# Attention of a hybrid block: one pipeline over pairs of heads, V as the stationary side

## What is computed

```python
scores = einsum('bqhgd,bkhd->bhgqk', qn, keys) - slopes * dist
scores = where(valid, scores, -inf)
m = maximum(max(scores, axis=-1), sink)
p = exp(scores - m)
probs = p / (sum(p, axis=-1) + exp(sink - m))
out = einsum('bhgqk,bkhd->bqhgd', probs, vals)

merged = (sigmoid(gr) * (y_ret @ w_ret_branch) + sigmoid(gs) * (y_swa @ w_swa_branch))
```

## Time and profile before

| | us |
|---|---|
| median of the runs | 1774.69 |
| lowest, highest of 3 | 1774.11, 1777.1 |
| the profiled execution: whole | 1776.14 |
| the profiled execution: first to last instruction (span) | 1774.6 |
| PE busy (share) | 1731.8 (98%) |
| DVE busy | 966.0 (54%) |
| ACT busy | 723.5 (41%) |
| POOL busy | 183.2 (10%) |

### The profile page before, as it was taken

The page is one execution under the profiler, slowest core; times in us unless marked ns, Lnnn a source line. Parts: engine busy times, 40 slices in busy tenths (PEclk is TensorE's granted clock), DMA queues, the critical chain, the costliest instruction groups (busy, mean ns, idle before and its releaser), DMA issues.

```text
span 1774.6 us, 24247 instructions
## 1 busy us (share of the span) xinstructions
PE 1731.8 (98%) x8504; PEld 1434.5 (81%) x8504; DVE 966.0 (54%) x1844; ACT 723.5 (41%) x1519; POOL 183.2 (10%) x329
## 2 busy tenths in 40 slices
PE   7999999999999999999999999879999989999999
PEld 6777888888778888888888788668888878888887
DVE  4311246522366666675556434766666645765776
ACT  5322345423255444444312213555455454444443
POOL 1000010100000000000222100112122122200000
PEclk9999999999999999999999999999999999999999
DMA  5111113211111111111555312244344349843363
GB/s 189 48 48 49 47 57 116 88 63 48 31 53 46 58 43 58 40 63 39 187 176 190 119 60 83 83 135 150 136 171 150 137 156 355 269 158 100 117 193 101
DMA packets 90580, 195.67 MB, mean 110 GB/s; under 512 B 10481, under 2 KB 26929, under 8 KB 90481
## 3 DMA queue, kind: packets, MB, share of 16 engines
q1 hardware_dynamic: 62432, 100.68, 18.0%
q0 software_dynamic: 28048, 93.74, 15.0%
HBM read 139.69 MB, written 54.53 MB: 109 GB/s over the span
## 4 chain that ended last, share of the span: by engine, by line
PE 91%; DVE 4%; DMA 2%; ACT 2%; issue 1%; SPq 0%; ACTq 0%; DVEq 0%
PE bank L585 26%; PE bank L590 26%; PE bank L589 26%; PE bank L848 4%; PE bank L809 2%; PE bank L842 1%; DMA RAW<-in_w_in 1%; DVE WL L1428 1%; PE bank L828 1%; PE bank L830 1%; DVE SOPL L1853 1%; PE bank L765 1%; PE bank L621 0%; PE bank L616 0%; PE bank L713 0%
## 5 line engine op out<-in xcount | busy, mean ns | idle before, releaser
L1428 DVE TENSOR_TENSOR WL<-RAW,WH 128x512 fp32r<-128x512 f32 x152 | 99.5, 688 | 153.3 <-ACT WH L1034 152.5
L585 PE MATMUL bank<-WH,HN 128*128 128x512 f32 x448 | 177.2, 395 | 4.0 <-DVE HN L1453 2.4
L585 PE MATMUL bank<-WH,ADH 128*128 128x512 f32 x448 | 175.4, 392 | 5.6 <-DVE WL L1994 5.6
L590 PE MATMUL bank<-WL,HN 128*128 128x512 f32 x448 | 175.4, 392 | 0.0
L589 PE MATMUL bank<-WH,HN 128*128 128x512 f32 x448 | 175.4, 391 | 0.0
L589 PE MATMUL bank<-WH,ADL 128*128 128x512 f32 x448 | 175.1, 391 | 0.0
L590 PE MATMUL bank<-WL,ADH 128*128 128x512 f32 x448 | 175.0, 391 | 0.0
L585 PE MATMUL bank<-HN,WH 128*128 128x512 f32 x384 | 157.3, 410 | 1.0 <-DVE WL L1428 1.0
L590 PE MATMUL bank<-HN,WH 128*128 128x512 f32 x384 | 150.8, 393 | 0.0
L589 PE MATMUL bank<-HN,WL 128*128 128x512 f32 x384 | 150.3, 391 | 0.0
L1403 ACT CAST ADH<-ARAW 128x512 fp32r<-128x512 f32 x112 | 69.5, 621 | 173.3 <-PE bank L590 171.0
(11 more groups left out here) (281 smaller groups left out, 3744.4 us busy)
## 6 DMA issues: line engine op xcount, KB each, us to landing
ARAW<-uop SPq DMA_DIRECT2D x112, 256.0 KB, 3.4
RAW<-in_w_in SPq DMA_DIRECT2D x104, 256.0 KB, 3.0
WRAW<-in_w_up SPq DMA_DIRECT2D x16, 1024.0 KB, 5.4
uop<-US POOLq DMA_DIRECT2D x64, 256.0 KB, 2.7
gates<-TB POOLq DMA_DIRECT2D x48, 256.0 KB, 2.3
uop<-UA POOLq DMA_DIRECT2D x48, 256.0 KB, 2.3
TH<-gates POOLq DMA_DIRECT2D x32, 256.0 KB, 3.0
RAWD<-in_w_down SPq DMA_DIRECT2D x32, 256.0 KB, 4.2
```

What stands on the lines that cost most here:

```text
L585: mm = pe.matmul(bank, ahi, bhi, start=first, stop=False, skip_group_check=onto)
L590: return pe.matmul(bank, ahi, blo, start=False, stop=last, skip_group_check=onto)
L1428: dve.tensor_tensor(WL[:, k, :], RAW[:, k % 4, :], WH[:, k, :].bitcast(F32), ALU.subtract)\
```

## The change

The attention becomes one pipeline over all 64 pairs of heads (8 blocks of 8), in 67 steps `T`, written out without loops; the 256 dense gate steps are spread evenly, 3 or 4 per step. Pair `T` gets its scores at the end of PE's step `T`, is transposed in step `T+2`, and pairs are multiplied with V in twos (a group of 4 heads) in every even step, two to three steps after.

- Scores and maximum: `tensor_tensor_reduce` (DVE) adds the distance to the scores, scales by the negated slope and takes the minimum with the negated sink in one instruction for each head (and a short one that reads the accumulator). POOL writes the sink beside the scores (`set_sink`), so that ACT's exponential sums it in with the rest. DVE takes the reciprocal, and POOL multiplies the weights by it (`tensor_scalar`, two of 272 columns) before they are transposed.
- Product with V: `KVR` holds V of a head group as 64 high and 64 low channels, 128 stationary columns. The moving side is the transposed weights of 4 heads, 512 columns, as a high part `PTH` (ACT) and a low part `PTL` (DVE), so 2 matmuls for each block of keys, float32r. The meta keys take 2 matmuls of 256 columns, 64 rows.
- y comes with channels on partitions. ACT copies bank 7 to `YA`; SP copies the upper half to its place in `RT`, and an accumulating POOL transfer adds the lower half. The 64 transposes of y are gone.
- Q and K of the next block are transposed group by group (4 and 2 transposes at a time, into bank 5).
- V of all blocks has to be split: a 256-column copy (ACT) and a subtraction (DVE) more in each block.

```diff
+STEPS = NPAIR + 3
+def gate_steps(T):
+    return range(4 * KT * 8 * T // STEPS, 4 * KT * 8 * (T + 1) // STEPS)
...
+            for T in range(STEPS):
+                for slab, k in ((SLAB_D, KT - 1),) if T == 0 else new_slabs(T - 1):
+                    load_block(8 * slab + k + 4)
+                if T >= 4 and T % 2 == 0:
+                    G = (T - 4) // 2
+                    sp.wait_ge(ya_rdy, G + 1)
+                    for par in range(2):
+                        sp.dma_start(y_place(G, par), y_part(G, 0, par)).then_inc(yc_done[G % 2], 16)
+            for slab, k in new_slabs(STEPS - 1):
+                load_block(8 * slab + k + 4)
...
+            def set_sink(T):
+                if T >= 3:
+                    pool.wait_ge(e_rdy, T - 2)
+                p = T % 8
+                pool.tensor_copy(PR[:, T % 3, 0:PRW:PRW - 1], NSK[:, 2 * p:2 * p + 2]).then_inc(sk_set, 1)
...
+            for T in range(STEPS + 2):
+                for i in gate_steps(T - 1) if 1 <= T <= STEPS else ():
...
+                    set_sink(T + 1)
+                if 1 <= T <= NPAIR:
+                    b = (T - 1) % 3
+                    pool.wait_ge(rc_rdy, T)
+                    for hl in range(2):
+                        pr = pool.tensor_scalar(PR[:, b, PR_KEYS[hl]], PR[:, b, PR_KEYS[hl]], RC[:, b, hl:hl + 1], None,
+                                                ALU.mult)
+                    pr.then_inc(pn_rdy, 1)
+                if T >= 6 and T % 2 == 0:
+                    G = (T - 6) // 2
+                    pool.wait_ge(yc_done[G % 2], 32 * (G // 2 + 1))
+                    for par in range(2):
+                        pool.dma_start(y_place(G, par), y_part(G, 1, par), accum_op=ALU.add)\
+                            .then_inc(yf_done[G % 2], 16)
...
+            def transpose_p(pair):
+                n, b = pair // 8, pair % 3
+                pe.wait_ge(pn_rdy, pair + 1)
+                if pair >= 1:
+                    pe.wait_ge(pl_rdy, split_of(pair - 1))
...
+            def values(G):
+                n, g = G // 4, G % 4
+                if G == 0:
+                    pe.wait_ge(mvb_done, 64)
+                pe.wait_ge(ql_rdy, 2 * n + 2)
+                pe.wait_ge(pl_rdy, meta_of(G))
+                if G >= 1:
+                    pe.wait_ge(ya_rdy, G)
+                for par in range(2):
+                    pe.matmul(B[7][:, :].rearrange("p (r a t) -> p r a t", r=2, a=2)[:, :, par, :],
+                              MVB[0:HD, par, g * P:(g + 1) * P],
+                              PTM[0:HD, :].rearrange("p (r t) -> p r t", r=2), start=par == 0, stop=True,
+                              skip_group_check=par == 1)
+                for sl in slots_of(n):
+                    v = KVR[:, n if sl == n % 2 else n - 1, g * P:(g + 1) * P]
+                    for part, tile in enumerate((PTH, PTL)):
+                        mm = pe.matmul(B[7][:, :], v, tile[:, sl, :, :].rearrange("p h t -> p (h t)"), start=False,
+                                       stop=True, skip_group_check=True)
+                mm.then_inc(pv_full, 1)
...
+            for T in range(STEPS):
+                for i in gate_steps(T):
+                    gate_step(i)
+                if T >= 4 and T % 2 == 0:
+                    values((T - 4) // 2)
+                if 2 <= T < NPAIR + 2:
+                    transpose_p(T - 2)
+                if T in NEXT_Q:
+                    transpose_next_q(*NEXT_Q[T])
+                if T in NEXT_K:
+                    transpose_next_k(*NEXT_K[T])
+                if T < NPAIR:
+                    scores(T)
...
+            def take_p(pair):
+                n, G = pair // 8, pair // 2
+                act.wait_ge(pt_full, pair + 1)
+                if pair % 2 == 0 and G >= 1:
+                    act.wait_ge(pv_full, G)
+                act.copy(pair_part(PTH, n, pair), pair_bank(n)).then_inc(ph_rdy, 1)
+                if pair % 2 == 1:
+                    act.copy(PTM[0:2 * META, :], B[6][0:2 * META, 0:2 * P]).then_inc(ph_rdy, 1)
+            def take_y(G):
+                act.wait_ge(pv_full, G + 1)
+                if G >= 2:
+                    act.wait_ge(yf_done[G % 2], 32 * (G // 2))
+                act.copy(YA[G % 2][:, :], B[7][:, :]).then_inc(ya_rdy, 1)
+            def weigh(T):
+                p = T % 8
+                act.wait_ge(sk_set, T + 1)
+                for hl in range(2):
+                    act.wait_ge(nm_rdy, 2 * T + hl + 1)
+                    part = PR[:, T % 3, hl * (NKEY + 1):(hl + 1) * (NKEY + 1)]
+                    e = act.activation(part, part, ACT.Exp, scale=-1.0, bias=NM[:, T % 3, hl:hl + 1],
+                                       accum_out=RS[:, T % 3, hl:hl + 1])
+                e.then_inc(e_rdy, 1)
+            for T in range(STEPS):
+                for i in gate_steps(T):
+                    if i % 8 == 7:
+                        c = i // 8
+                        g = tanh_gate(ACT_D + c, c % 8, 8 + c // 2)
+                        g.then_inc(a_free if c < 16 else th_rdy, 1)
+                if 2 <= T < NPAIR + 2:
+                    take_p(T - 2)
+                if T >= 4 and T % 2 == 0:
+                    take_y((T - 4) // 2)
+                if T % 8 == 2 and T // 8 + 1 < NB:
+                    hi_q(T // 8 + 1)
+                if T % 8 == 3 and T // 8 + 1 < NB:
+                    hi_kn(T // 8 + 1)
+                if T in NEXT_Q:
+                    take_next_q(*NEXT_Q[T])
+                for slab, k in new_slabs(T):
+                    split_hi(slab, k)
+                if T < NPAIR:
+                    weigh(T)
...
+            def top(T):
+                n, p = T // 8, T % 8
+                if p == 0:
+                    dve.wait_ge(dt_full[n % 2], 16 * (n // 2 + 1))
+                if T >= 3:
+                    dve.wait_ge(pt_full, T - 2)
+                for hl in range(2):
+                    hh = 2 * p + hl
+                    dve.wait_ge(sc_full, 2 * T + hl + 1)
+                    dve.tensor_tensor_reduce(PR[:, T % 3, PR_KEYS[hl]], B[2 + hl][:, 0:NKEY], DT[:, n % 2, KEYS_OF[hl]],
+                                             -SLOPES[hh], NSK[:, hh:hh + 1], ALU.add, ALU.min,
+                                             NM[:, T % 3, hl:hl + 1]).then_inc(nm_rdy, 1)
+            def lo_p(pair):
+                n, G = pair // 8, pair // 2
+                dve.wait_ge(ph_rdy, split_of(pair))
+                dve.tensor_tensor(pair_part(PTL, n, pair), pair_bank(n), pair_part(PTH, n, pair).bitcast(F32), ALU.subtract)\
+                   .then_inc(pl_rdy, 1)
+                if pair % 2 == 1:
+                    dve.wait_ge(ph_rdy, meta_of(G))
+                    dve.tensor_tensor(PTM[2 * META:4 * META, :], B[6][0:2 * META, 0:2 * P],
+                                      PTM[0:2 * META, :].bitcast(F32), ALU.subtract).then_inc(pl_rdy, 1)
+            for T in range(STEPS):
+                if T < NPAIR:
+                    top(T)
+                if 2 <= T < NPAIR + 2:
+                    lo_p(T - 2)
+                if T % 8 == 0 and T // 8 + 1 < NB:
+                    normed_qk(T // 8 + 1)
+                if T % 8 == 2 and T // 8 + 1 < NB:
+                    lo_q(T // 8 + 1)
+                if T % 8 == 3 and T // 8 + 1 < NB:
+                    lo_kn(T // 8 + 1)
+                if T in NEXT_K:
+                    take_next_k(*NEXT_K[T])
+                for i in gate_steps(T):
+                    if i % 8 == 7 and i >= 128:
+                        c = i // 8
+                        dve.wait_ge(th_rdy, c - 15)
+                        dve.scalar_tensor_tensor(out=TB[:, c % 2, :], in0=TB[:, c % 2, :], scalar=1.0,
+                                                 in1=B[c % 2][:, :], op0=ALU.add, op1=ALU.mult).then_inc(a_free, 1)
+                for slab, k in new_slabs(T):
+                    split_lo(slab, k)
+                if T < NPAIR:
+                    dve.wait_ge(e_rdy, T + 1)
+                    dve.reciprocal(RC[:, T % 3, :], RS[:, T % 3, :]).then_inc(rc_rdy, 1)
...
-            def transpose_ys(b, u, bank):
-                for k in range(4):
-                    mm = pe.transpose(bank[:, k * P:(k + 1) * P], RT[:, u, b, k * P:(k + 1) * P], IDN[:, :])
-                mm.then_inc(st_full, 1)
...
+            def hi_ys(b, u):
+                for par in range(2):
+                    act.wait_ge(yf_done[par], 32 * (2 * b + u + 1))
                 act.copy(YS[b // 4][:, 0, 4 * u:4 * u + 4, (b % 4) * P:(b % 4 + 1) * P],
-                         bank[:, :].rearrange("p (k t) -> p k t", k=4)).then_inc(sh_rdy, 1)
+                         RT[:, u, b, :].rearrange("p (k t) -> p k t", k=4)).then_inc(sh_rdy, 1)
             for u in range(2):
```

More of the change, by code:

```diff
@@ L47, with new_slabs, split_of, meta_of @@
 START = 1
-KS_D = [[0, 1, 2], [3, 4, 5], [6, 7]]
+NPAIR = 8 * NB
+NG = NPAIR // 2
+STEPS = NPAIR + 3
+NEXT_Q = {8 * (m - 1) + 2 * g + 3: (m, g) for m in range(1, NB) for g in range(4)}
```

(41 more changed lines are left out.)

470 lines of the change are left out of this document (182 added, 288 removed).

## The result

The changed kernel takes 1746.80 us, median of 4 runs (1745.42 to 1747.64), against 1774.54 for the kernel before: ratio 0.984, 95% interval 0.9823 to 0.9857. That is 27.7 us less, where 44.5 were forecast. It lies 0.2 us inside the upper end of the range (1747), and two of the four runs lie beyond it. Its profiled execution has a span of 1744.6 us, 30.0 less.

What follows compares the result with a forecast made beforehand. PE's work was taken to bound the kernel: 1774.7 us, less 58.6 of PE's work, plus 14.1 of waits for other engines, gave 1730.2 us, with a range of 1714 to 1747.

Steps and rivals of the forecast that it cites:

- dearer DVE: Rival, chance 0.20: `tensor_tensor_reduce` takes two cycles a column, 1.6 us a pair, adding 10 us, so 1740.
- Product with V: PE's attention stage: 64 pairs at 1.41 us go, 32 groups at 1.25 come; net -52.0 us.
- Waits: PE waiting for other engines in the attention stage: Q's split, slab changes and small ones, +14.1 us.
- Splitting Q: ACT and DVE finish splitting the next Q after PE wants it, in 7 blocks: 4.5 us of waits.
- Slab changes: Around steps 16, 32 and 48 DVE's extra work makes PE wait: 8.9 us together.
- Scores: A gate matmul now always follows a pair's last score matmul, saving 0.11 us in each of 64: -7.0 us.
- transposes of block 0: Block 0 leaves out two transposes a pair on PE: -1.5 us.
- Q and K pieces: PE's 24 transposes of Q and K a block come in 8 pieces instead of 2: +3.8 us.
- End of the stage: PE idles 6.1 us instead of 4.1 before the branch projection, behind weight tiles and casts of y: +2.0 us.
- PE never waits: Rival, chance 0.22: DVE's pieces are shorter or waits fall where PE had slack, so 1716 us.
- The accumulating transfer: Rival, chance 0.04: POOL's transfer of y lands after 8.8 us, holding up ACT's `take_y`; at 13 us, 1797.
- POOL's pace: Rival, chance 0.06: POOL's multiplication takes 2.5 us or more, steps 5.5 us and more, so 1750 to 1775.

Runs made afterwards that it cites:

- Experiment 2: Changed kernel with the meta part's two matmuls with V over 128 rows (64 to 127 zero) instead of 64: 1737.7 us, ratio 0.9786.
- experiment 1: Changed kernel with DVE's copy of the next block's transposed K moved to the start of its step: 1740.3 us, ratio 0.9801.
- Experiment 3: Changed kernel with the first half's casts and subtractions of y ahead of the stage's last three weight tiles on ACT and DVE: 1747.3 us, ratio 0.983.
- experiment 4: Changed kernel with POOL's second multiplication, for the odd heads' weights, left out: 1745.8 us, ratio 0.9828.
- Experiments 7 and 11: First, the changed kernel with scores and maximum in separate instructions: 1766.1 us. Second, the kernel before with only the fused instruction: 1775.6 us against 1776.0.
- experiment 6: Changed kernel with the K copy ahead of the maxima, meta matmuls over 128 rows, and the next Q split in two halves: 1725.0 us, ratio 0.9719.
- experiment 10: Changed kernel with POOL's 64 accumulating transfers of y made plain ones, without the sum of the halves: 1749.3 us, one run.

## Why the prediction came out as it did

The mechanism was right: PE's work set the time, V's product was most of the gain, and waits ate a part. The time came out 16.6 us above the forecast. That it is still inside the range, by 0.2 us, is luck: the range reached to 1747 for a dearer DVE, and DVE wasn't dearer. Step by step, for the stage:

- **Product with V, forecast -52.0.** A group costs 1.54, not 1.25: +9.3. The step that failed is "two of 256 columns at 0.12 (the neighbours in the retention stage start 0.12 apart)". Those have 128 rows, the new ones 64, and I took the price over without the row count. Experiment 2 shows it: with 128 rows a group costs 1.16.
- **Waits, forecast +14.1, measured some 21.2** (late starts against the usual distance). "Splitting Q 4.5" was right in size: 4.2 was left once the K copy was out of the way. "Slab changes 8.9" was too large: there and at POOL's weights PE lost 5.3. What was missing is the copy of K, some 8 us (experiment 1). I had counted its 0.4 us in DVE's sums, but asked only when the next product with V could start, not who waits for each thing that DVE does last. PE needs bank 5 back at S + 3.2, when it comes to the transposes of Q, and on DVE the copy stands behind the maxima, `PTL` and Q's work. A further 1.9 went at the first scores, where PE waits for ACT's `QT`, and 1.4 by a lower clock after two waits, below.
- **Scores -7.0, transposes of block 0 -1.5:** right, by 0.59 against 0.58 a step. **Q and K pieces, +3.8:** they cost 4 x 0.38 + 4 x 0.21 = 2.4 a block where the kernel before took some 2.1, so +1.8; 2.0 too much. The 1.6 us that PE itself waited in the old stage also went, and I hadn't counted it.
- **End of the stage, +2.0:** the idle time is 8.04, not 6.1. The three weight tiles weren't 0.55 each: ACT waited 1.1, 0.6 and 0.7 for their loads. Experiment 3 shows this.

The sum: +9.3 + 7.1 + 1.9 - 2.0 - 1.6 = 14.7, for 14.0 that are missing. Behind the stage I had 3.9 from the transposes of y; the span gives 3.4, though the projection starts at half the clock (1.9 us lost, below), so something there is some 1.4 better than forecast; what it is stays open.

**The rivals.** PE never waits: wrong, as argued from step 32, though for the wrong wait. Dearer DVE at 1740: the pair took 0.85, even less than my 1.0, so the time in that rival's range has another cause. The accumulating transfer landed in 2.9 us, far from the 8.8 from which it would count, and ACT's copy of bank 7 never waits for it. POOL's pace: it was busy 3.3 us a step and stayed under the 5 of a step, and with half of its arithmetic gone nothing is gained (experiment 4). Of what the profile was to show, "PE busy some 94 to 97%" came out at 93% (310.72 of 334.85) and "PE waiting for `QST`, `PTL` and `WL`, most around the three slab changes" only in part: more than half of the waiting is at line 956, spread over the blocks. "V's 512-column matmuls at another distance than 0.23" was the sign to look for, and it was there for the first of each group.

**Whose gain it was.** Experiments 7 and 11 answer what no sum over one trace does. The fused instruction is worth nothing in the kernel before and 17.6 to 19.3 us in the changed one; the other parts alone are worth some 10. The forecast had it right that DVE's shorter step buys nothing while PE is full, and used it only as a smaller term in the waits. It is rather what lets the rest of the change show most of its gain.

## What to carry to other kernels

When PE's share is cut, list for each resource that PE reuses (a bank, a buffer) who gives it back and where that stands in the giver's queue: a 0.4 us copy late in DVE's step cost some 8 us until it was moved to the front. Take the price of a matmul from a row with the same number of rows as well as columns; padding a 64-row product with zeros to 128 rows made it cheaper here. And price an edit within the whole: one that is worth nothing alone can carry another.

## What the hardware showed that was not expected

- **64 rows cost more than 128.** Two 256-column matmuls took 0.43 us with 64 rows and 0.24 with 128, and the matmuls next to them lost 0.09 to 0.10 each; at both changes the weight load started with its matmul instead of 0.22 or 0.12 ahead of it (experiment 2).
- **The clock after short gaps.** After PE's 8.04 us idle the granted clock was down to its lower level, 1.2 GHz, for about 4 us: eight matmuls stand 0.43 apart instead of 0.23, and with the first one behind the gap 1.9 us are lost. 3.72 us of idle did the same in experiment 3, from 1.0 us behind the restart. Two waits of 1.66 and 1.74 us at 742 to 745 us also brought it:

```profile
742.61 0.66 PE L926 MATMUL bank<-IDN,PR 128*128 128x128 f32 x4 [1.66 <-POOL PR L583]
...
745.12 0.51 PE L956 MATMUL bank<-IDR,QST 128*128 128x128 f32 x4 [1.74 <-DVE KTS L1746]
...
746.25 0.63 PE L697 MATMUL bank<-HN,WH 128*128 128x512 f32 x1
746.67 0.63 PE L701 MATMUL bank<-HN,WL 128*128 128x512 f32 x1
```

  A wait of about 2 us ahead of the first scores was followed by it in experiment 6 (2.00 us idle, granted clock 0.50 from 493 to 495 us) and not in experiment 2 (2.03 us idle, 1.00). So a wait can cost more than its length, and shortening the gap at the end of the stage from 8.0 to 3.7 us saved only some 0.2 of the 1.9 us.
- **POOL.** A multiplication of 272 columns by one factor per row took 0.95 us from start to start, 3.5 ns a column, where the two-input addition of 512 in the earlier trace rows takes 2.5 ns a column. An accumulating transfer has a record of 1.16 us against 0.62 for a plain one, and the records behind it are longer as well, but POOL's next instructions start as early behind it (1.24 us for two against 1.23), and it lands in 2.9 us against 2.0 (experiment 10). Take the price of a POOL transfer from start to start, as with matmuls.
